# 48 tokens gathered in place of 32, eleven gathers begun in the u pass, gates and first products packed in DRAM by pair of expert tiles

## The chip, the cores and the metric

The kernel runs on one core of a Trainium2 chip. The metric is the device time of one execution in microseconds (us); the time of a kernel is the median of its runs. All data is float32; matrix products run in TensorE's fp32r form with each operand split into a high and a low part, so that one product of full precision is three matmuls (high x high, high x low, low x high).

## What is computed

Two transformer blocks over 256 tokens of width 2048. The change touches only the feed-forward part of the first, a PEER layer with 16384 experts (128 x 128 keys), of which each token picks 128 (8 heads, top 16 of each) with a gate:

```
def peer(xn, wq, subkeys, u, v):
    ...
    idx = e1 * PEER_NKEYS + e2
    gate = jax.nn.softmax(sc, axis=-1).astype(xn.dtype)
    ...
        h = jax.nn.gelu(jnp.einsum('cd,chkd->chk', xc, u[ic]))
        return jnp.einsum('chk,chkd->cd', gc * h, v[ic])
```

`u` and `v` are 16384 x 2048 each, 134 MB each.

## The kernel before

**Two ways through the experts.** Most tokens (`DENSE`, 224 of 256) are done densely. In the *u pass* the 128 tiles of `u` (128 experts each, 1 MB) are multiplied with all dense tokens (`expert_hidden`), the result goes through gelu and to DRAM (`hidden_dram`). In the *v pass* it comes back, is multiplied by a dense table of gates that is zero where an expert was not picked (`weigh`), split into high and low, and multiplied with the 128 tiles of `v` (`expert_mix`). The last `GATHERED` = 32 tokens are done sparsely: their 32 x 128 (token, expert) pairs are laid on 128 partitions, four copies of the 32 tokens, so that 32 *units* of 128 pairs cover them. For each unit GpSimd issues indirect DMAs which fetch 128 rows of `u` (1 MB), VectorE takes the dot product with the token's row (`unit`, L1901, with an accumulator), ScalarE the gelu of all of them (L2689), and then 32 more units fetch rows of `v` and add them, weighted, to `gathered_sum` (L1911). At the end four fp32 matmuls with a 0/1 matrix (`copies_summed`) add the copies into the PSUM banks of the v pass. All 64 units run in the v pass.

**The stream.** SyncE loads weights in halves of a tile (512 KB) into two raw buffers of two halves. ScalarE makes the high part of a half (L2322), VectorE the low part (L1353), into four buffers each; both work three halves ahead of TensorE (`LOOKAHEAD`), and SyncE reloads a half when its low part is done. A half of the u pass is 8 matmuls with a high part as weights and the high and low activations of the dense tokens as moving columns (2 x `DENSE` = 448), then 8 with a low part and the high activations alone (224). A half of the v pass is 12 matmuls of 512 columns whose weights are 128 tokens of the weighed products; the width there does not depend on `DENSE`, since rows up to 256 are filled with zeros.

**Stages of the u pass.** Every engine runs a program in fixed order. In tiles 0 to 47 (`CHOICE_QUADS` = 12 quads of four tiles) VectorE does the top-16 choices between its splits (`choose`, `top16`, `advance`). From tile 48 on, one tile at a time, the dense gates are made, 4 tokens per tile, `GATE_QUADS` = `DENSE` / 16 = 14 quads: VectorE compares indices with iota (`onehots`, L1819, L1822), ScalarE scales the result (`gate_first`, L2599), TensorE multiplies four pairs of one-hot matrices (`gates`), ScalarE and VectorE copy and add the result into `gates_out` (L2607, L1854). The order of VectorE within such a tile is: low part, `sum_hidden` (L1689, every other tile), `sum_gates` of the tile before, `onehots` of the tile after, low part. ScalarE's is: high part, first product or gelu, `copy_gates`, high part, `gate_first` of the tile after, and in some tiles a store of gates. `gates_out` holds two quarters of 64 tokens; each quarter is stored in 8 DMAs, one per tile. The tail of the u pass, tiles 104 to 127, has neither choice nor gates, only the stores of the last quarter in its first eight tiles. When all are stored, GpSimd loads a gain row to all partitions, four copies of the 32 tokens' rows, and the final gain (L2912 to L2915).

**Placement of units.** GpSimd starts a piece of a gather when TensorE is done with a given half (`piece_half`), four pieces of 256 KB per unit; VectorE does unit `u` after the splits of tile `unit_tile(u)`, one unit in 1.8 tiles. There are three gather buffers.

Of the kernel before, what the change touches and what calls it, by code (L numbers as in the profile page):

```python
# [34 lines left out]
P = 128  # L35
# [78 lines left out]
def build(nc, ins, out):  # L114
    ctx = ExitStack()
    with ctx:
# [137 lines left out]
        pair_scale = r_pairs.take(1)  # L254
        r_pairs.take(1)
        copies_summed = r_pairs.take(P)
# [3 lines left out]
        gates_out = r3.take(2 * EXPERT_TILES * QUARTER, "p (b e t) -> p b e t", b=2, t=QUARTER)  # L260
        onehots_at = big_at + 4 * r3.at
# [9 lines left out]
        r3_mix = Region(D)  # L271
        hidden_in = r3_mix.take(2 * N, "p (b n) -> p b n", b=2)
        gates_in = r3_mix.take(2 * N, "p (b q e t) -> p b q e t", b=2, q=T // QUARTER, e=2)
        weighed = r3_mix.take(N)
# [4 lines left out]
        gathered_x = r3_mix.take(D)  # L279
        gathered_rows = r3_mix.take(UNIT_BUFFERS * D, "p (b d) -> p b d", b=UNIT_BUFFERS)  # L280
        gathered_sum = r3_mix.take(D)
        assert r3_mix.at <= 20512
# [4 lines left out]
        gates_dram = nc.dram_tensor("gates_dram", [T // QUARTER, P, EXPERT_TILES, QUARTER], F32)  # L287
        hidden_dram = nc.dram_tensor("hidden_dram", [EXPERT_TILES // 2, P, N], F32)
# [294 lines left out]

        def piece_half(m):

            return 2 + 9 * m // 10

        def unit_tile(u):

            return (piece_half(UNIT_PIECES * u + UNIT_PIECES - 1) + 1) // 2 + 2  # L590

        units_at = {unit_tile(u): u for u in range(UNIT_TILES)}
        assert len(units_at) == UNIT_TILES and max(units_at) < EXPERT_TILES - 2
        dots_tile = unit_tile(UNITS_G - 1) + 1
        assert dots_tile < unit_tile(UNITS_G)
# [6 lines left out]
        def _(sp):  # L602
# [22 lines left out]
            def store_hidden(n, j):  # L625

                sp.wait_ge(gelu_done, 2 * n + (j + 1 + PRIMED))
                sp.dma_start(hidden_dram[bass.ds(2 * n + j, 1)].rearrange("a p n -> p (a n)"), hidden[:, j, :]
                             ).then_inc(hidden_stored[j], 16)

            def load_mix(n, j):
# [6 lines left out]
                sp.dma_start(gates_in[:, j, :, :, :], gates_dram[:, :, bass.ds(4 * n + 2 * j, 2), :].rearrange("q p e t -> p q e t")  # L638
# [50 lines left out]
        def _(pe):  # L689
# [637 lines left out]
        def _(dve):  # L1327
# [555 lines left out]
            for j in range(4):  # L1883
                if j % 2 == 0:
                    sum_hidden(EXPERT_QUADS - 1, j // 2 - 1)
# [1163 lines left out]
```

## Time and profile before

| | |
|---|---|
| median of 3 runs | 2964.53 us (2963.01 to 2964.64) |
| profiled execution, its own time | 2963.21 us |
| its span, first to last instruction | 2961.4 us |
| TensorE busy | 2929.9 us (99%), 16686 matmuls |
| VectorE busy | 2141.8 us (72%) |
| ScalarE busy | 1530.3 us (52%) |
| GpSimd busy | 398.6 us (13%) |
| moved by DMA | 684.56 MB, 231 GB/s on average |
| u pass | from about 437 us to 1128 us |
| v pass | from 1128 us to about 1829 us |

The end of a matmul is modelled and includes its way through the array, so that consecutive matmuls overlap; the pace of TensorE is read from the distance of starts. The share of a DMA window is the time in which an engine has a packet; it can be near 1 before the bytes per second are at their highest.

### The profile page before, as it was taken

The page shows a single profiled execution, that of the slowest core. Times are in us where ns is not written, and L with a number is a line of the kernel's source. Part 1 is how long each engine was busy: PE and PEld are TensorE (multiplying, and loading weights), DVE is VectorE, ACT ScalarE, POOL GpSimd, SP SyncE. Part 2 cuts the span into 40 slices and gives each one's busy share as a digit, 9 for nine tenths or more (in the row PEclk, how much of TensorE's full clock was granted, in tenths as well). Part 3 has the DMA queues.
Part 4 walks back from the last instruction along what each step waited for, and adds up shares of the span by engine and source line. Part 5 has one row for each costly group of instructions (what it writes and reads, how often), then busy time and mean ns, then how long its engine had stood idle before and what let it go on. Part 6 is the DMA issues. An engine that isn't in the chain of part 4 may idle for free.

```text
span 2961.4 us, 46358 instructions
## 1 busy us (share of the span) xinstructions
PE 2929.9 (99%) x16686; PEld 2573.7 (87%) x16686; DVE 2141.8 (72%) x2739; ACT 1530.3 (52%) x2120; POOL 398.6 (13%) x315
## 2 busy tenths in 40 slices
PE   8999999999999999999999999999999999999999
PEld 8887999899999998888888887978889888888887
DVE  5776689977999756777777776775666776777444
ACT  4565534566777644444444444444545555555333
POOL 2000000000000003556556640000000000000000
PEclk9999999999999999999999999999999999999999
DMA  8444546676777989999999995545455555556555
GB/s 285 137 142 149 180 157 208 216 243 213 244 246 255 329 289 317 347 346 351 348 345 346 346 341 173 175 140 171 156 185 183 180 190 192 184 185 196 194 179 184
DMA packets 232763, 684.56 MB, mean 231 GB/s; under 512 B 25613, under 2 KB 62686, under 8 KB 232000
## 3 DMA queue, kind: packets, MB, share of 16 engines
q1 hardware_dynamic: 199552, 583.09, 59.4%
q0 software_dynamic: 23664, 78.15, 7.5%
q10 hardware_dynamic: 9440, 21.93, 2.1%
q8 instruction: 63, 1.03, 0.1%
q14 instruction: 44, 0.36, 0.0%
HBM read 646.28 MB, written 36.49 MB: 231 GB/s over the span
## 4 chain that ended last, share of the span: by engine, by line
PE 84%; DVE 8%; ACT 4%; DMA 2%; issue 2%; ACTq 0%; POOL 0%; SPq 0%; DVEq 0%; POOLq 0%
PE bank L693 83%; DVE low L1353 3%; ACT high L2322 2%; DMA raw<-in_experts_u_t 2%; DVE onehots_both L1819 1%; ACT first_both L2599 1%; PE bank L984 0%; DVE big L1854 0%; DVE big L1698 0%; DVE big L1702 0%; DVE big L1697 0%; DVE big L1689 0%; DVE big L1700 0%; PE bank L783 0%; DMA big<-in_c_onehot_cmp 0%
## 5 line engine op out<-in xcount | busy, mean ns | idle before, releaser
L1353 DVE TENSOR_TENSOR low<-raw,high 128x1024 fp32r<-128x1024 f32 x1008 | 1230.5, 1223 | 655.2 <-ACT high L2322 652.7
L2322 ACT ACTIVATE high<-raw 128x1024 fp32r<-128x1024 f32 x1008 | 1061.3, 1057 | 998.4 <-PE bank L693 901.0
L693 PE MATMUL bank<-act_both,high 128*128 128x448 f32 (+2 forms) x5088 | 1119.3, 348 | 10.9 <-DVE low L1353 8.1
L693 PEld LDWEIGHTS bank<-act_both,high 128*128 128x128 f32 x5088 | 875.7, 190 | 94.0 <-issue 12.9
L693 PE MATMUL bank<-act_both,low 128*128 128x256 f32 (+1 forms) x4240 | 697.1, 278 | 0.0
L693 PEld LDWEIGHTS bank<-act_both,low 128*128 128x128 f32 x4240 | 615.8, 191 | 21.2
L693 PE MATMUL bank<-high,weighed_high 128*128 128x512 f32 x1024 | 399.0, 390 | 0.5 <-DVE weighed_low L1836 0.4
L693 PE MATMUL bank<-high,weighed_low 128*128 128x512 f32 x1024 | 398.4, 389 | 0.0
L693 PE MATMUL bank<-low,weighed_high 128*128 128x512 f32 x1024 | 398.4, 389 | 0.0
L693 PE MATMUL bank<-high,act_both 128*128 128x512 f32 (+1 forms) x960 | 308.7, 392 | 1.4 <-ACT big L2491 1.4
L693 PEld LDWEIGHTS bank<-high,weighed_high 128*128 128x128 f32 x1024 | 192.2, 188 | 41.0 <-issue 1.3
L693 PEld LDWEIGHTS bank<-high,weighed_low 128*128 128x128 f32 x1024 | 192.2, 188 | 40.2
L693 PEld LDWEIGHTS bank<-low,weighed_high 128*128 128x128 f32 x1024 | 192.2, 188 | 39.9 <-issue 0.2
L693 PEld LDWEIGHTS bank<-high,act_both 128*128 128x128 f32 x960 | 180.1, 188 | 37.7 <-issue 1.9
L2927 POOL DMA_INDIRECT big<-in_experts_u,big x128 | 181.3, 1417 | 215.5 <-PE bank L693 199.3
L2927 POOL DMA_INDIRECT big<-in_experts_v_t,big x128 | 188.2, 1470 | 125.3 <-PE bank L693 109.4
L693 PE MATMUL bank<-low,act_both 128*128 128x512 f32 (+1 forms) x480 | 185.4, 386 | 0.0
L693 PE MATMUL bank<-high,ff_high 128*128 128x512 f32 x352 | 137.2, 390 | 0.0
L693 PE MATMUL bank<-low,ff_high 128*128 128x512 f32 x352 | 137.0, 389 | 0.0
L693 PE MATMUL bank<-high,ff_low 128*128 128x512 f32 x352 | 136.9, 389 | 0.0
L2599 ACT ACTIVATE first_both<-onehots_both,taps 128x128 fp32r<-128x128 f32 x224 | 71.8, 391 | 76.3 <-DVE onehots_both L1819 76.3
L693 PE MATMUL bank<-big 128*32 128x128 f32 (+11 forms) x860 | 103.1, 324 | 7.1 <-DMA big<-in_c_onehot_cmp 1.7
(304 smaller groups left out, 2202.2 us busy)
## 6 DMA issues: line engine op xcount, KB each, us to landing
raw<-in_experts_u_t SPq DMA_DIRECT2D x256, 512.0 KB, 4.9
raw<-in_experts_v_t SPq DMA_DIRECT2D x256, 512.0 KB, 6.1
raw<-in_w_up_t SPq DMA_DIRECT2D x176, 512.0 KB, 4.6
raw<-in_w_in_t SPq DMA_DIRECT2D x136, 512.0 KB, 4.0
raw<-in_w_down_t SPq DMA_DIRECT2D x88, 512.0 KB, 4.7
raw<-in_w_out_t SPq DMA_DIRECT2D x64, 512.0 KB, 3.8
raw<-in_peer_wq_t SPq DMA_DIRECT2D x32, 512.0 KB, 3.7
hidden_dram<-big SPq DMA_DIRECT2D x64, 256.0 KB, 3.8
```

The costliest lines, as they stand in the source:

```text
L693: return pe.matmul(out_, lhs_t, rhs, start=start, stop=stop, skip_group_check=True)
L1353: dve.tensor_tensor(low[b][:, :], raw[r][:, HALF * which:HALF * (which + 1)], as_f32(high[b][:, :]), ALU.subtract).then_inc(low_ready[b], 1)
L1819: dve.tensor_tensor(onehots_both[:, c, :, :, :], row(picked_t[:, 0:2, bass.ds(token, FOUR)], P), copies(copies(iota[:, :], FOUR), 2), ALU. ...
L2322: act.activation(high[b][:, :], raw[r][:, HALF * which:HALF * (which + 1)], ACT.Copy).then_inc(high_ready[b], 1)
L2599: m = act.activation(first_high[:, c, t, :], first[:, c, t, :], ACT.Copy, scale=picked_t[:, 2, bass.ds(4 * FOUR * n + (FOUR * j + t), 1)])
L2927: pool.indirect_dma_start(out=gathered_rows[:, b, D // UNIT_PIECES * piece:D // UNIT_PIECES * (piece + 1)], out_offset=None, in_=rows_of, ...
```

## The change

`DENSE` becomes 208, `GATHERED` 48 in two groups: 32 tokens in four copies and 16 tokens in eight copies, each with its own copy of the tokens' rows (`gathered_x`), its own sum and its own 0/1 matrix. That makes 48 units of `u` and 48 of `v`, 96 in place of 64. `GATE_QUADS` becomes 13. A unit is gathered in two pieces of 512 KB. Of the units of `u`, up to `UNIT_TAIL` = 12 are placed in the tail of the u pass, in two of three tiles from tile 110; the list that the expression gives has eleven entries (110, 111, 113, 114, 116, 117, 119, 120, 122, 123, 125). The other 85 go to tiles 1 to 123 of the v pass. In DRAM the first products and the gates lie by pair of expert tiles, 416 floats in a row for each partition. The loads of the token rows and of the gain row come before the tail's units, and the load of the final gain (1 MB) behind unit 35.

```diff
-GATHERED = 32
+TOKEN_GROUPS = [32, 16]
+GATHERED = sum(TOKEN_GROUPS)
 DENSE = T - GATHERED
-COPIES = P // GATHERED
-UNITS_G = P // COPIES
+UNITS_G = GATHERED
 UNIT_BUFFERS = 3
-UNIT_PIECES = 4
+UNIT_PIECES = 2
+UNIT_FROM, UNIT_TAIL = 109, 12
...
+        gathered_x = [Region(0).take(D), Region(r3.at).take(D)][:len(TOKEN_GROUPS)]
...
-        gates_dram = nc.dram_tensor("gates_dram", [T // QUARTER, P, EXPERT_TILES, QUARTER], F32)
-        hidden_dram = nc.dram_tensor("hidden_dram", [EXPERT_TILES // 2, P, N], F32)
+        gates_dram = nc.dram_tensor("gates_dram", [EXPERT_TILES // 2, P, 2 * DENSE], F32)
+        hidden_dram = nc.dram_tensor("hidden_dram", [EXPERT_TILES // 2, P, 2 * DENSE], F32)
...
+        tail_tiles = [t for t in range(UNIT_FROM, EXPERT_TILES - 2) if t % 3 != UNIT_FROM % 3][:UNIT_TAIL]
+        UNITS_V = UNIT_TILES - len(tail_tiles)
...
+            if u < len(tail_tiles):
+                return tail_tiles[u]
+            return EXPERT_TILES + 1 + u // UNITS_G + (u - len(tail_tiles)) * (EXPERT_TILES - 5) // UNITS_V
+
+        def unit_half(u, piece):
+
+            h = 2 * unit_tile(u) - 5 + piece * 2 // UNIT_PIECES
+            return half("experts_u_t", h) if h < 2 * EXPERT_TILES else half("experts_v_t", h - 2 * EXPERT_TILES)
...
-                    for q in range(4):
-                        mm(bank[:, 4 + q, :], copies_summed, gathered_sum[:, N * q:N * q + N], start=False, stop=False)
+                    for g in range(len(TOKEN_GROUPS)):
+                        for q in range(4):
+                            mm(bank[:, 4 + q, :], copies_summed[:, g, :], gathered_sum[g][:, N * q:N * q + N], start=False, stop=False)
...
+            def gather_step(tile):
+
+                if UNIT_FROM - 2 <= tile < UNIT_FROM - 2 + len(TOKEN_GROUPS):
+                    g = tile - (UNIT_FROM - 2)
+                    dve.wait_ge(subkeys_rows_gain_landed, 16 * (2 + X_LOADS))
+                    dve.tensor_tensor(gathered_x[g], gathered_x[g], gathered_rows[:, UNIT_BUFFERS - 1, :], ALU.mult
+                                      ).then_inc(gathered_x_ready, 1)
...
-                act.dma_start(gates_dram[q, :, at, :], gates_out[:, q % 2, at, :]).then_inc(gates_stored[q % 2], 16)
+                tokens = quarter_tokens(q)
+                to = gates_dram[EXPERT_TILES // 2 // GATE_PIECES * piece:EXPERT_TILES // 2 // GATE_PIECES * (piece + 1), :,
+                                2 * QUARTER * q:2 * (QUARTER * q + tokens)]
+                act.dma_start(to.rearrange("a p n -> p a n"),
+                              gates_of(q)[:, at, :].rearrange("p (a e) t -> p a (e t)", e=2)).then_inc(gates_stored[q % 2], 16)
...
-            for b in range(2):
-                pool.wait_ge(gates_stored[b], 16 * GATE_PIECES * 2)
+            pool.wait_ge(gates_stored[0], 16 * GATE_PIECES * 2)
             pool.dma_start(gathered_rows[:, UNIT_BUFFERS - 1, :], ins["ffn_norm"].partition_broadcast(P)).then_inc(subkeys_rows_gain_landed, 16)
...
+            for c in range(SLOTS):
+                pool.wait_ge(gates_done[c], 2 * GATE_QUADS + PRIMED)
+            for g, tokens in enumerate(TOKEN_GROUPS):
+                for r in range(P // tokens):
+                    pool.dma_start(gathered_x[g][tokens * r:tokens * (r + 1), :], resid[group_at[g]:group_at[g] + tokens, TT - 1, :]
+                                   ).then_inc(subkeys_rows_gain_landed, 16)
```

## Rows read from the trace of the kernel before

**Rows 1.** The chain that ended last, by line, share of the span.

```profile
PE bank L693 83%; DVE low L1353 3%; ACT high L2322 2%; DMA raw<-in_experts_u_t 2%; DVE onehots_both L1819 1%; ACT first_both L2599 1%; PE bank L984 0%; DVE big L1854 0%; DVE big L1698 0%; DVE big L1702 0%; DVE big L1697 0%; DVE big L1689 0%; DVE big L1700 0%; PE bank L783 0%; DMA big<-in_c_onehot_cmp 0%
```

**Rows 2.** Windows: stretch, length; busy us of PE, PEld, DVE, ACT, POOL; clock; DMA share; GB/s.

```profile
561.00:617.00 56.00, 56.00 (x358) 53.20 (x357) 55.17 (x51) 35.73 (x39) 0.00 (x0) 1.00 0.73 232
617.00:697.00 80.00, 80.00 (x509) 76.00 (x508) 47.05 (x52) 49.47 (x59) 5.91 (x12) 1.00 0.75 241
...
698.00:1002.00 304.00, 304.00 (x1983) 289.87 (x1982) 275.88 (x301) 224.97 (x437) 0.00 (x0) 1.00 0.75 249
...
1030.00:1045.00 15.00, 15.00 (x97) 14.24 (x96) 9.05 (x10) 8.82 (x10) 0.00 (x0) 1.00 1.01 387
...
1060.00:1075.00 15.00, 12.92 (x74) 12.02 (x73) 6.39 (x6) 7.16 (x9) 0.00 (x0) 0.89 0.93 313
...
1075.00:1125.00 50.00, 50.00 (x319) 47.49 (x318) 29.34 (x28) 25.93 (x31) 0.00 (x0) 1.00 0.80 263
...
1140.00:1450.00 310.00, 310.00 (x1369) 256.68 (x1369) 238.98 (x233) 135.49 (x143) 179.26 (x127) 1.00 0.98 348
```

**Rows 3.** Timeline of TensorE: start, us, operation, times, in five short stretches.

```profile
902.36 0.65 PE L693 MATMUL bank<-first_both,onehots_both 128*128 128x256 f32 x4
902.85 1.79 PE L693 MATMUL bank<-act_both,high 128*128 128x448 f32 x8
...
1107.48 1.80 PE L693 MATMUL bank<-act_both,high 128*128 128x448 f32 x8
1109.12 1.04 PE L693 MATMUL bank<-act_both,low 128*128 128x224 f32 x8
1110.01 1.80 PE L693 MATMUL bank<-act_both,high 128*128 128x448 f32 x8
...
1819.59 3.60 PE L693 MATMUL bank<-big 128*128 128x512 f32 x8
...
1978.60 1.95 PE L693 MATMUL bank<-big 128*128 128x64 f32 x16
```

**Rows 4.** Timeline of all engines in the choices: a low part and the half that uses it.

```profile
565.87 1.22 DVE L1353 TENSOR_TENSOR low<-raw,high 128x1024 fp32r<-128x1024 f32 x1
...
568.78 0.38 PE L693 MATMUL bank<-act_both,high 128*128 128x448 f32 x1
```

**Rows 5.** Timeline of all engines in the gate tiles; in brackets idle before, and releaser.

```profile
698.12 0.64 PE L693 MATMUL bank<-first_both,onehots_both 128*128 128x256 f32 x4
698.24 1.22 DVE L1819 TENSOR_TENSOR onehots_both<-taps,iota 128x1024 fp32r<-128x1024 f32 x1
...
703.64 0.65 PE L693 MATMUL bank<-first_both,onehots_both 128*128 128x256 f32 x4
...
904.12 1.22 DVE L1819 TENSOR_TENSOR onehots_both<-taps,iota 128x1024 fp32r<-128x1024 f32 x1
...
905.37 0.41 ACT L2599 ACTIVATE first_both<-onehots_both,taps 128x128 fp32r<-128x128 f32 x1 [1.14 <-DVE onehots_both L1819]
...
906.56 1.04 ACT L2322 ACTIVATE high<-raw 128x1024 fp32r<-128x1024 f32 x1
...
907.64 1.23 DVE L1353 TENSOR_TENSOR low<-raw,high 128x1024 fp32r<-128x1024 f32 x1 [0.33 <-ACT high L2322]
...
909.91 1.22 DVE L1819 TENSOR_TENSOR onehots_both<-taps,iota 128x1024 fp32r<-128x1024 f32 x1
...
999.17 1.22 DVE L1819 TENSOR_TENSOR onehots_both<-taps,iota 128x1024 fp32r<-128x1024 f32 x1
...
1002.05 0.65 PE L693 MATMUL bank<-first_both,onehots_both 128*128 128x256 f32 x4
```

**Rows 6.** DMA issues of 1045 to 1062 us: queue, times, KB each, us to landing.

```profile
raw<-in_experts_u_t SPq DMA_DIRECT2D x5, 512.0 KB, 14.6
...
big<-in_final_norm POOLq DMA_DIRECT2D x1, 1024.0 KB, 19.1
```

**Rows 7.** Line L1901, VectorE's instruction of a unit of u: ns min/median/max.

```profile
L1901 DVE SCALAR_TENSOR_TENSOR big<-big x32: 2282/2284/2290, 1155.6 to 1460.3; 128x2048 f32<-128x2048 f32 x32
```

More of the change, by code:

```diff
@@ L1870, in _ @@
                 for j in range(4):
-                    gate_tile(q, n0, j, q if j else (q - 1 if q else None))
+                    gate_tile(q, n0, j, q if j else (q - 1 if q else None), last=n0 == GATE_QUADS - 1 and j == 3)
                 if not last_q:
@@ L1875, in _ @@
                             gate_tile(q, n, j, q)
-            assert GATE_QUADS == QUARTER_QUADS * (T // QUARTER - 1) + 2
-            for j in range(4):
-                gate_tile(T // QUARTER - 1, GATE_QUADS - 1, j, T // QUARTER - 1, last=j == 3)
+            for n in range(QUARTER_QUADS * (T // QUARTER - 1) + 1, GATE_QUADS):
+                for j in range(4):
+                    gate_tile(T // QUARTER - 1, n, j, T // QUARTER - 1, last=n == GATE_QUADS - 1 and j == 3)
             sum_gates(T // QUARTER - 1, GATE_QUADS, -1)
-            with dve.Fori(0, EXPERT_QUADS - CHOICE_QUADS - GATE_QUADS - 1) as n:
-                for j in range(4):
-                    split_tile_low("experts_u_t", n + (CHOICE_QUADS + GATE_QUADS), j)
@@ L1883, in _ @@
-            for j in range(4):
-                if j % 2 == 0:
-                    sum_hidden(EXPERT_QUADS - 1, j // 2 - 1)
-                split_low(half("experts_u_t", 2 * j + LOOKAHEAD, EXPERT_QUADS - 1))
-                if j == 3:
-                    weigh_low(0, 0)
-                split_low(half("experts_u_t", 2 * j + LOOKAHEAD + 1, EXPERT_QUADS - 1))
-                if j == 2:
-                    weigh(0, 0)
-            sum_hidden(EXPERT_QUADS - 1, 1)
             def unit(u):
-                b, used = u % UNIT_BUFFERS, u // UNIT_BUFFERS
+                b, used, column = u % UNIT_BUFFERS, u // UNIT_BUFFERS, u % UNITS_G
@@ new lines, in _ @@
+            for tile in range(4 * (CHOICE_QUADS + GATE_QUADS), EXPERT_TILES):
+                n, j = tile // 4, tile % 4
+                if n < EXPERT_QUADS - 1:
+                    split_tile_low("experts_u_t", n, j)
+                else:
+                    if j % 2 == 0:
+                        sum_hidden(n, j // 2 - 1)
+                    split_low(half("experts_u_t", 2 * j + LOOKAHEAD, n))
+                    if j == 2:
+                        dve.wait_ge(gates_stored[1], 16 * GATE_PIECES * 2)
+                        for ap in (weighed_high, weighed_low):
+                            dve.memset(as_f32(ap.rearrange("p b (e t) -> p (b e) t", e=2)[:, :, DENSE:]), 0.0)
+                    elif j == 3:
+                        weigh_low(0, 0)
+                    split_low(half("experts_u_t", 2 * j + LOOKAHEAD + 1, n))
+                    if j == 2:
+                        weigh(0, 0)
+                gather_step(tile)
@@ L1914, in _ @@
+            sum_hidden(EXPERT_QUADS - 1, 1)
             for n in range(EXPERT_QUADS):
```

150 lines of the change are left out of this document (82 added, 68 removed).

## The prediction

> **What bounds the kernel now.** I read the chain of work first: 83% of it is one line, TensorE's matmul helper, and the next, VectorE's low part, has 3% [rows 1]. Then windows by stage. From 561 us to the end of the v pass TensorE is busy in practically every microsecond [rows 2], so a shorter matmul can pay, but only where nobody else stands close behind. Who does is read from VectorE and DMA in the same windows: VectorE is busy 55.17 of 56 us at the end of the choices, 47.05 of 80 after them, 275.88 of 304 in the gate tiles; DMA is at 0.75 in the gate tiles, at 1.01 and 387 GB/s while the last quarter of gates is stored, and at 0.98 and 348 GB/s in the v pass [rows 2]. One stretch lost time: 1060 to 1075, TensorE busy 12.92 of 15 and the clock at 0.89, part of it at 1.2 in place of 2.4 GHz. That is 2.1 us idle and 0.11 x 15 = 1.7 us of clock, 3.8 us, just after GpSimd's loads of the two gain rows and the tokens' rows (1 MB each): the weight halves beside it took 14.6 us to land [rows 6]. The timeline of TensorE gives the price of a half, the timeline of all engines the gate tiles.
>
> **The matmuls of the u pass.** A half starts at 1107.48, its low part at 1109.12, the next half at 1110.01 [rows 3]: 1.64 us for 8 matmuls of 448 columns (205 ns each), 0.89 us for 8 of 224 (111 ns), 2.53 us in all; the long run of the gate tiles, below, gives 2.518. The change makes them 416 and 208. The wide ones should follow their columns: 32 columns at 2.4 GHz are 13.3 ns, 8 x 13.3 = 0.107 us per half. The narrow ones may not. Elsewhere 16 matmuls of 64 columns with a full 128x128 weight take 1.95 us [rows 3]; less some 0.27 for the way of the last one through the array that is 1.68 / 15 = 112 ns each, though their columns are 27 ns (the same sum for the narrow ones: (1.04 - 0.27) / 7 = 110). The 224-column ones pass at the same 111 ns. So some 110 ns looks like what it takes to change weights, and 208 columns save nothing. The ends: 0 (the 64-column row) and 16 columns = 6.7 ns x 8 = 0.053 us per half. I take 0, since two widths so far apart share one pace. Saved per half: 0.107 us, 27 us over 256 halves if TensorE alone set the pace.
>
> The Trainium skill, page "TensorE: Matmul & The Clock Gate", section "LDWEIGHTS (loading the stationary operand)", says the same: a weight load takes time by its 128 columns, 128 / 1.2 = 107 ns, whatever streams past. The section "Back-to-back issue gap" of that page prices an isolated gap by the columns alone, and by it the narrow matmuls would save too.
>
> **Choices, tiles 0 to 47.** Up to about 617 us VectorE has no idle time [rows 2] and its program doesn't get shorter but for the sums of first products (448 to 416 columns, under 1 us together). TensorE can't be ahead of it. It can only eat its lead: the low part that ends at 565.87 + 1.22 is used at 568.78, 1.7 us later [rows 4]. After 617, 32 halves at 0.107 are 3.4 us. Gain: 1.7 + 0.6 + 3.4 = 5.7.
>
> **Gate tiles.** This is where I expect most of the gain to vanish. There TensorE takes 5.526 us per tile: (1002.05 - 703.64) / 54 [rows 5], which is two halves and 0.49 for the four gate matmuls (902.36 to 902.85 [rows 3]), so 2.518 for a half. VectorE's one-hot comparisons go at (999.17 - 698.24) / 54 = 5.573 us [rows 5], slower than TensorE. Their lead over the gate matmuls that use them falls from 703.64 - 698.24 = 5.40 to 1002.05 - 999.17 = 2.88 us. What drives them is a loop of VectorE and ScalarE in which TensorE has no part: comparison at 904.12, ScalarE waited 1.14 us for it and starts the scaled copies at 905.37, then its high part at 906.56, VectorE waited 0.33 for that and makes the low part at 907.64, adds, and compares again at 909.91 [rows 5]. Nothing in this loop shrinks but the add of first products (0.03 us every other tile: 0.017 per tile). The lead can't fall below comparison plus copies, about 2.5 us. So 52 tiles take 52 x 5.556 less the 2.9 us of lead, 286.0, against 52 x 5.526 = 287.4 before: a gain of 1.4, where TensorE alone would gain 52 x 2 x 0.107 = 11.1. The other bound is that the loop has slack that I don't see: 11.1. I take 1.4, because in that window no wait of VectorE or ScalarE on TensorE stands against the loop. The four tiles that lose their gates go from 5.526 to 2 x (2.518 - 0.107) = 4.82: 2.8. The 32 stores of gates remain 32; those of q 0 to 2 go in rows of 512 B, the last in rows of 128 B. Their issue lies in that loop (some 0.1 us), 20 in place of 24 inside the stage.
>
> **Tail, the 24 tiles from 104.** 48 x 0.107 = 5.1. VectorE takes on a unit of 2.28 us [rows 7] in 11 tiles; with two splits of 1.23 and half a sum it is at some 5.0 us in such a tile of 4.83 and 2.8 in the third, which its lead hides. The two products with the gain row, once under the v pass, are now at tiles 107 and 108, and VectorE waits there for 1 + 12 loads of GpSimd. These start when the store of tile 103 has landed, about 5 us into tile 104, and move 3 MB like the cluster before, whose last load took 19.1 us [rows 6]; with 12 issues I put the end at 26.6 us after the start of tile 104. VectorE arrives at 19.2. Behind the wait are the low parts of half 219 and on: 26.6 + 2.28 + 1.23 = 30.1 against the 26.6 at which TensorE wants it. 3.5 us idle, and a clock fall like that of 1060 (1.7): 5.2 in place of the 3.8 us lost before. Bounds: 0 (landing early) to 10. Then the gathers: per tile of 4.83 us 1.05 MB of weights, 0.11 of first products, two thirds of 1.05 of rows: 1.85 MB, 384 GB/s, where the nearest stretch had 387 at a share of 1.01 [rows 2]. That is the edge; I count 2.5 us, from 0 to 6.3 (at 348 / 0.98 = 355 GB/s a tile takes 5.22, 0.39 x 16). Sum of the tail against before: 5.1 - (5.2 + 2.5 - 3.8) = +1.2.
>
> **The v pass.** Its 3072 matmuls keep their form: 0. Twenty-one units more (85 for 64) are 21 x 2.3 = 48 us of VectorE's time, which has 71 us idle in 310 [rows 2]: hidden; the smaller weigh operations pay for their second instruction. If the cover is gone the low parts come late, at most by one unit. GpSimd issues 192 gathers for 256. DMA: in 10.88 us (two tiles) weights 2.10 MB, packed operands 0.43 for 0.52, rows 1.45 for 1.17: 365 GB/s for 348. Larger rows than 512 B speak for it, the share of 0.98 against. I count 1 us lost, between 0 and 19 (355 GB/s: 2.8% of 684 us). The load of the final gain, 1 MB alone, is hidden. At the end 4 fp32 matmuls more: eight records at 0.43 us make four of them [rows 3], 3.4 us on the path.
>
> **Sum.** 5.7 + 1.4 + 2.8 + 1.2 - 1 - 3.4 = 6.7 us off the profiled execution's own 2963.2 (span 2961.4), 2956.5. The median of the runs is 1.3 above that execution, so 2957.8; I say 2958.
>
> **The rivals.**
>
> DMA is the limit (slower). Place: tail and v pass; it decides as soon as the kernel can't be served over 355 GB/s for long. The tail loses 3.8 more, the v pass 19 in place of 1: 2958 + 22 = 2980. For it: shares of 0.98 to 1.01 at 348 to 387 GB/s. Against: the share is full long before the bytes stop rising (387), and TensorE never waited in the v pass. The middle of this case is 2970, half of it within 0.2% of before. The Trainium skill, page "DMA: Bandwidth & Descriptors", section "Where 436 GB/s comes from", puts the HBM side of one core at some 358 GB/s, and by it this case would come about; its section "Measured (HBM→SBUF, 128 partitions, SWDGE, issued from GpSimd)" has 425 for one core alone, and the row with 387 sides with that.
>
> The gate loop isn't binding: +9.7, 2948. For it: TensorE was never idle there. Against: the falling lead [rows 5].
>
> The narrow matmuls follow their columns: 0.053 x (32 + 56 halves) = 4.7: 2953.
>
> No larger stall: loads land before tile 107 and the gathers fit: up to 7.7 less, 2951.
>
> The change does nothing in sum: 2964.5, inside the spread of the above.
>
> **How the numbers follow.** Forecast case (2953 to 2964) 0.45, gate loop or columns 0.17, no stall 0.13, DMA 0.25. A measurement here can tell 0.2%, 5.9 us. Faster by more than that (under 2958.6): 0.5 of the first, all of the next two: 0.52. Within: 0.45 of the first and half of the DMA case: 0.33. Slower: 0.15. The range leaves out the upper part of the DMA case and little below: 2946 to 2974; the forecast's own is 2953 to 2964.
>
> **What would show it.** Halves in the tail start every 2.41 us, with 8 narrow matmuls still at 0.11 (2.36 would be the other case). In the gate tiles TensorE's period stays near 5.55 and it waits for the low part or for the one-hots, in all about 10 us. TensorE idle once near tile 107 with VectorE waiting on a DMA. GB/s near 380 in the last 16 tiles of the u pass. v pass from first matmul to last still about 701 us plus 3.4. I am wrong if gate tiles take 5.32, or the v pass grows by more than 8 us.

## The result and the profile after

The changed kernel takes 2996.05 us (median of 4 runs, 2990.71 to 2998.17) against 2964.59 us (4 runs, 2963.01 to 2964.68): a ratio of 1.0104, 95% interval 1.0092 to 1.0115. It is 31 us slower, where I had said 6.5 us faster. Its profiled execution took 2998.17 us, with a span of 2996.4 us.

I laid the two traces over each other by the starts of the 256 halves of the u pass and of the 3072 matmuls of the v pass. "Ahead" is how much earlier the changed kernel gets there.

| point | before, us | after, us | ahead | predicted |
|---|---|---|---|---|
| tile 48 (half 96), end of the choices | 693.08 | 686.49 | 6.6 | 5.7 |
| tile 100 (half 200), end of its gate tiles | 980.36 | 972.96 | 7.4 | 7.1 |
| tile 104 (half 208) | 1002.53 | 992.37 | 10.2 | 9.9 |
| tile 109 (half 218) | 1027.83 | 1016.50 | 11.3 | 10.9 |
| tile 110 (half 220) | 1032.88 | 1039.09 | -6.2 | not told apart |
| first matmul of the v pass | 1127.96 | 1128.61 | -0.6 | 8.7 |
| last matmul of the v pass | 1829.16 | 1864.16 | -35.0 | 4.3 |

So the change works as foreseen for 109 tiles, loses 17.5 us between the halves of tiles 109 and 110, gets 5.6 of that back by the end of the u pass (the kernel before has its own stall there [rows 2]), and loses 34 us in the v pass.

The chain that ended last, by line, shows only that time went to other places than before [rows 1]:

```profile
PE bank L714 64%; DVE low L1375 4%; DMA raw<-in_experts_v_t 3%; DMA raw<-in_experts_u_t 1%; ACT high L2359 1%; DVE big L1922 1%; DMA big<-resid 1%; DVE big L1911 1%; PE bank L1005 0%; DVE big L1720 0%; DVE big L1724 0%; DVE big L1719 0%; DVE big L1722 0%; DVE big L1801 0%; DVE big L1803 0%
```

Windows of the changed kernel (columns as in [rows 2]):

```profile
698.00:992.00 294.00, 290.64 (x1922) 284.35 (x1921) 261.19 (x286) 214.35 (x412) 0.00 (x0) 1.00 0.77 251
1006.00:1012.00 6.00, 6.00 (x43) 5.97 (x42) 4.52 (x6) 3.43 (x5) 6.00 (x13) 1.00 1.06 327
1012.00:1018.00 6.00, 6.00 (x40) 5.96 (x39) 0.00 (x0) 1.34 (x2) 3.07 (x4) 1.00 1.06 289
1018.00:1024.00 6.00, 1.07 (x9) 0.89 (x8) 0.00 (x0) 1.06 (x1) 0.94 (x1) 0.82 1.04 219
1024.00:1030.00 6.00, 0.00 (x0) 0.00 (x0) 0.00 (x0) 0.00 (x0) 0.00 (x0) 0.50 1.02 218
1075.00:1125.00 50.00, 48.55 (x317) 47.60 (x316) 40.37 (x41) 25.35 (x30) 14.80 (x11) 1.00 0.94 341
1140.00:1450.00 310.00, 305.51 (x1303) 245.91 (x1303) 241.84 (x267) 128.54 (x139) 109.74 (x74) 0.99 0.96 352
```

From 1018 to 1030 nearly everything stands still at a DMA share over 1.0 and only 218 GB/s; the clock falls from 2.4 to 1.2 GHz (0.50) as TensorE stands. Timeline of all engines around it (matmuls left out but for the first after the stall):

```profile
997.53 0.38 ACTq L2672 DMA_DIRECT2D gates_dram<-big  x1
...
1005.84 0.54 POOL L2963 DMA_DIRECT2D big<-in_ffn_norm  x1 [365.82 <-DMA gates_dram<-big]
1006.37 5.78 POOL L2968 DMA_DIRECT2D big<-resid  x12
...
1010.61 1.23 DVE L1375 TENSOR_TENSOR low<-raw,high 128x1024 fp32r<-128x1024 f32 x1 [0.40 <-ACT high L2359]
...
1022.84 1.06 ACT L2359 ACTIVATE high<-raw 128x1024 fp32r<-128x1024 f32 x1 [9.51 <-DMA raw<-in_experts_u_t]
...
1030.54 2.29 DVE L1930 TENSOR_TENSOR big<-big 128x2048 f32<-128x2048 f32 x1 [18.71 <-DMA big<-resid]
...
1034.65 1.75 PE L714 MATMUL bank<-act_both,high 128*128 128x416 f32 x4 [15.58 <-DVE low L1375]
```

The reader is to see four times: the last store of the gates of quarter 2 issued at 997.53, GpSimd let go by it at 1005.84, VectorE done with everything ahead of the x step at 1011.84, and the x step at 1030.54. The DMA view of 1006 to 1030 says what was in flight (KB each, median us to landing):

```profile
raw<-in_experts_u_t SPq DMA_DIRECT2D x3, 512.0 KB, 17.6
big<-in_ffn_norm POOLq DMA_DIRECT2D x1, 1024.0 KB, 8.6
big<-resid POOLq DMA_DIRECT2D x4, 256.0 KB, 11.0
big<-resid POOLq DMA_DIRECT2D x8, 128.0 KB, 15.9
gates_dram<-big ACTq DMA_DIRECT2D x3, 128.0 KB, 26.5
```

In the v pass the first thing to see is the pace. Timeline of TensorE in the kernel before, then in the changed one:

```profile
1240.25 0.39 PE L693 MATMUL bank<-high,weighed_high 128*128 128x512 f32 x1
...
1241.61 0.39 PE L693 MATMUL bank<-high,weighed_high 128*128 128x512 f32 x1
```

```profile
1239.62 0.39 PE L714 MATMUL bank<-high,weighed_high 128*128 128x512 f32 x1
...
1241.02 0.39 PE L714 MATMUL bank<-high,weighed_high 128*128 128x512 f32 x1
```

Six matmuls take 1.36 us before (227 ns each) and 1.40 after (233 ns), nobody waiting. An undisturbed v tile of 24 takes 5.44 us before and 5.57 to 5.60 after, from the first tile to the last: about 18 us over the pass. The second thing is some ten gaps of 0.5 to 3 us each between pairs of tiles, 12 to 13 us in sum. Some 3 us of that are clock and not waiting: behind the gaps at tiles 36 and 86 seven matmuls each start 0.43 us apart, and the granted clock is 0.50 (1.2 GHz) from 1337 to 1339 us, after TensorE had stood for 2.57 us. The third was foreseen: the fp32 matmuls, now sixteen records in 7.03 us against eight in 3.60 [rows 3].

### The profile page after: what moved, and what is told of

It is laid out like the page before. It is cut to its first block, busy times and chain, and to the rows that moved or that the text cites. A ratio compares the mean times of both kernels' runs of the same rounds, so it can differ in the third digit from the quotient of the medians.

```text
span 2996.4 us, 46333 instructions
## 1 busy us (share of the span) xinstructions
PE 2935.5 (98%) x16678; PEld 2579.6 (86%) x16678; DVE 2191.0 (73%) x2842; ACT 1515.1 (51%) x2101; POOL 345.7 (12%) x283
## 3 DMA queue, kind: packets, MB, share of 16 engines
q0 software_dynamic: 31856, 112.76, 10.4%
## 4 chain that ended last, share of the span: by engine, by line
PE 66%; issue 14%; DVE 10%; DMA 6%; ACT 2%; POOL 1%; SPq 1%; ACTq 0%; DVEq 0%; POOLq 0%
PE bank L714 64%; DVE low L1375 4%; DMA raw<-in_experts_v_t 3%; DMA raw<-in_experts_u_t 1%; ACT high L2359 1%; DVE big L1922 1%; DMA big<-resid 1%; DVE big L1911 1%; PE bank L1005 0%; DVE big L1720 0%; DVE big L1724 0%; DVE big L1719 0%; DVE big L1722 0%; DVE big L1801 0%; DVE big L1803 0%
## 5 line engine op out<-in xcount | busy, mean ns | idle before, releaser
L714 PE MATMUL bank<-act_both,high 128*128 128x416 f32 (+2 forms) x5088 | 1094.8, 343 | 29.0 <-DVE low L1375 25.3
L714 PE MATMUL bank<-high,weighed_high 128*128 128x512 f32 x1024 | 406.7, 397 | 8.4 <-DVE weighed_low L1860 8.3
L714 PE MATMUL bank<-high,weighed_low 128*128 128x512 f32 x1024 | 405.5, 396 | 0.0
L714 PE MATMUL bank<-low,weighed_high 128*128 128x512 f32 x1024 | 405.3, 396 | 0.0
L2983 POOL DMA_INDIRECT big<-in_experts_v_t,big x96 | 158.7, 1653 | 237.7 <-PE bank L714 212.8
L2983 POOL DMA_INDIRECT big<-in_experts_u,big x96 | 142.6, 1485 | 270.9 <-PE bank L714 256.4
L714 PE MATMUL bank<-big 128*32 128x128 f32 (+12 forms) x868 | 105.6, 324 | 6.9 <-ACT big L2427 1.6
L1911 DVE SCALAR_TENSOR_TENSOR big<-big 128x2048 f32<-128x2048 f32 x48 | 109.7, 2285 | 0.0
```

Of the source, the lines that this page charges most:

```text
L714: return pe.matmul(out_, lhs_t, rhs, start=start, stop=stop, skip_group_check=True)
L1911: dve.scalar_tensor_tensor(gathered_rows[:, b, :], gathered_rows[:, b, :], 1.0, gathered_x[g], ALU.mult, ALU.mult, accum_out=pair_dots[:, ...
L2983: pool.indirect_dma_start(out=gathered_rows[:, b, D // UNIT_PIECES * piece:D // UNIT_PIECES * (piece + 1)], out_offset=None, in_=rows_of, ...
```

## The experiments

Each ratio below is to the kernel before, run beside it on the same chip; its median there was 2962 to 2964 us.

**Place of the weight tiles.** `weighed_high` is what the v pass loads as weights, 128 columns (512 bytes) at a time. Its place in the tile `big` went from float 4608 to float 10272. The 6144 floats of the three gather buffers, which now lie ahead of it, change nothing in the remainder; the three operand tiles there, whose pairs went from 512 to 416 columns, do: 10272 floats are 41088 bytes, 128 past a multiple of 256. All such remainders here are counted from the start of `big`.

a1_align, the changed kernel:

```diff
         weighed = r3_mix.take(2 * DENSE)
+        r3_mix.take(480)
```

> The changed kernel with one edit: 480 floats are left free ahead of weighed_high, so that this tile starts at float 10752 of big (a multiple of 512 floats, as 4608 was in the kernel before) and not at 10272. Everything else, transfers and waits included, is that of the changed kernel. Theory 'place' (a weight tile that starts off a 512-byte boundary makes each v matmul start later): the interval between matmuls of the v pass goes back from about 232 ns to 227 ns, some 5 ns x 3072 = 15 us, so 2996 becomes about 2980; the stall near tile 108 of the u pass stays. Rival 'contention' (the larger gather rows and longer VectorE work share the memory with TensorE): the interval stays at 232 and the time at about 2996.

Measured: 2986.48 us (6 runs), 1.0081 (1.0067 to 1.0095). b1_shift32, the kernel before:

```diff
         weighed = r3_mix.take(N)
+        r3_mix.take(32)
```

> The kernel before with one edit: 32 floats are left free ahead of weighed_high, so that it starts at float 4640 of big and not at 4608, with the same remainder as in the changed kernel (128 bytes past a multiple of 512). Theory 'place': its v matmuls go from 227 ns to about 232 ns and its time from 2964.6 to about 2980. Rival 'contention': nothing in the traffic changes, so 227 ns and 2964.6 within 0.2%.

Measured: 2981.64 us, 1.0065 (1.0051 to 1.008). Timeline of TensorE in b1_shift32, then in a1_align:

```profile
1239.81 0.39 PE L694 MATMUL bank<-low,weighed_high 128*128 128x512 f32 x1
...
1241.20 0.39 PE L694 MATMUL bank<-low,weighed_high 128*128 128x512 f32 x1
```

```profile
1240.16 0.39 PE L715 MATMUL bank<-high,weighed_high 128*128 128x512 f32 x1
...
1241.52 0.39 PE L715 MATMUL bank<-high,weighed_high 128*128 128x512 f32 x1
```

1.39 us for six in the first, 1.36 in the second. The v pass of b1_shift32 is 719.9 us from first to last matmul, against 701.2: 32 empty floats cost 18.7 us, with not a byte of traffic changed and no wait of TensorE added. "Contention" is out. (`gathered_sum`, which lies behind the weight tiles, moved with them; e1 below rules it out.) a1_align has its 227 ns back, but not 15 us: its gaps grew. Its v pass is still 723.9 us. So a second cause is at work, stronger when TensorE is faster.

**Loads or gathers in the tail of the u pass, and where VectorE waits.** Both on a1_align:

```diff
 # a2_x_later
-UNIT_FROM, UNIT_TAIL = 109, 12
+UNIT_FROM, UNIT_TAIL = 115, 8
 # a3_no_tail
-UNIT_FROM, UNIT_TAIL = 109, 12
+UNIT_FROM, UNIT_TAIL = 109, 0
```

> The kernel of a1_align, and the x steps of VectorE moved from tiles 107 and 108 to tiles 113 and 114; 8 units remain in the tail of the u pass (tiles 115 to 125) in place of 12, the other 4 go to the v pass. The 13 loads that GpSimd issues stay where they are, after the gates are stored. Theory 'in-order wait' (VectorE stands 18.7 us behind those loads and the low halves queue behind it): the wait is gone or below 3 us, the u pass ends some 12 us earlier, about 12 us off a1_align's time. Rival 'the DMA engines themselves' (2 MB of x, 1 MB of gain, the last gate stores and the stream do not fit at once): ScalarE waits for raw in place of VectorE, TensorE stands still for 10 us or more between tiles 104 and 114 all the same, and at most 5 us come back.

> The kernel of a1_align with no unit in the tail of the u pass: all 96 units stand in the v pass, the x steps stay at tiles 107 and 108, and the first gathers are issued in the v pass. It tells the loads from the gathers. If the 13 loads and the gate stores make the stall, VectorE still waits over 12 us at tile 107 and TensorE loses about as much as before. If the four gathers issued right behind the loads make it, the wait falls to 5 us or less. The v pass then holds 96 units, about one in 1.3 tiles, at 2.3 us each beside a tile of 5.45 us of matmuls: if VectorE or the gathers were too much for a v tile, its tiles would pass 5.6 us.

(The program's rule leaves out every third tile and stops at tile 125, so that 11 of the 12 and 7 of the 8 units get a place in the tail. "84" and "88" units in the v pass are 85 and 89.)

a2_x_later: 2986.99 us, 1.0081 (1.0067 to 1.0096). Between halves 218 and 222 TensorE loses 8.7 us against the kernel before, where a1_align lost 15.1, now behind ScalarE's waits for raw; the u pass ends 4.6 us earlier than in a1_align, not 12. Both theories have a part of it: VectorE's standing cost some 6 us, the crowd at the DMA engines 9. The time is that of a1_align although the u pass gained 4.6 us: the v pass, with four units more, is 3.3 us longer (727.2 us).

a3_no_tail: 2999.78 us, 1.0129 (1.0114 to 1.0143). No gather is near, and the half at tile 110 still starts 15.9 us later against before than the one ahead of it: the gathers have no part in the stall. Windows of a3_no_tail:

```profile
1018.00:1024.00 6.00, 2.37 (x16) 2.17 (x14) 0.00 (x0) 1.06 (x1) 0.00 (x0) 1.00 1.05 241
1024.00:1030.00 6.00, 0.00 (x0) 0.00 (x0) 0.00 (x0) 1.06 (x1) 0.00 (x0) 0.56 0.98 232
```

The v pass with 96 units takes 734.9 us, 11 more than a1_align's with 85.

**Size of the gathers' pieces, tokens, bytes.** Edits of a1_align; c3_32_tokens has 320 in place of 480 floats, which puts `weighed_high` at the same float 10752.

```diff
 # c1_pieces4, c2_pieces1
-UNIT_PIECES = 2
+UNIT_PIECES = 4        # c2_pieces1: 1
 # c3_32_tokens
-TOKEN_GROUPS = [32, 16]
+TOKEN_GROUPS = [32]
-UNIT_FROM, UNIT_TAIL = 109, 12
+UNIT_FROM, UNIT_TAIL = 109, 0
 # c5_half_gather_v
-out=gathered_rows[:, b, D // UNIT_PIECES * piece:D // UNIT_PIECES * (piece + 1)],
+out=gathered_rows[:, b, D // UNIT_PIECES * piece:D // UNIT_PIECES * (piece + 1) - (512 if u >= UNITS_G + UNIT_BUFFERS else 0)],
```

> The kernel of a1_align with every gathered row fetched in 4 pieces of 2 KB, as in the kernel before, in place of 2 pieces of 4 KB. Same bytes, twice the packets of the gathers. Theory 'DMA rate' (84 units stand in the v pass where 64 stood; 1.97 MB a tile in 5.44 us is 362 GB/s, and a1_align moved 351 to 360 GB/s at a DMA share of 0.96 to 0.98, so the pieces of v arrive late and TensorE loses 19 us in some 12 places): with the rate of the kernel before, 346 to 349 GB/s at 0.98, each v tile would take 1.97 MB / 348 GB/s = 5.66 us, and the v pass would lose about 27 us and not 19: about 8 us slower than a1_align. Rival 'bursts' (a 0.5 MB piece holds back the stream's tile behind it): smaller pieces interleave better and 5 us or more come back.

> The kernel of a1_align with every gathered row fetched in one piece of 8 KB. 'DMA rate': somewhat fewer packets, so the same time as a1_align or up to 5 us less. 'Bursts': 1 MB at once holds back the stream twice as long; 5 us or more slower than a1_align.

> The changed code with 32 gathered tokens as before (64 units, all in the v pass, none in the tail), DRAM packed by pair of expert tiles, x loads and x step where the change has them (tiles 104 to 107 of the u pass), and weighed_high on a multiple of 512 floats. It is the packing, the larger pieces of 4 KB and the earlier x loads without the 16 tokens more. If the losses come from the 16 tokens (32 units more), the v pass takes 701 us as before, at a lower DMA share than 0.98, and the time is 2962 within 0.3%, a few us less if the early x step costs nothing; if the packing or the order of the tail makes them, it is 2970 or more.

> The kernel of a1_align, but from the 52nd unit on (tile 59 of the v pass) each piece fetches 2 KB of its 4 KB: it leaves out half of those rows' columns, which keep old values. VectorE's and GpSimd's instructions are the same in number and length. 'DMA bytes': up to tile 59 TensorE loses about 8 us as in a1_align, after it nothing but the 3.4 us of the four fp32 matmuls and the end (a1_align: 14 us), so about 10 us less in all. Rival 'VectorE' (units of 2.3 us in order ahead of the low halves): the stalls after tile 59 stay, 14 us.

| kernel | median, us | ratio (95%) | v pass, first to last matmul, us |
|---|---|---|---|
| a1_align, 2 pieces | 2986.48 | 1.0081 (1.0067 to 1.0095) | 723.9 |
| c1_pieces4 | 2970.88 | 1.0023 (1.0014 to 1.0033) | 711.5 |
| c2_pieces1 | 2993.84 | 1.0114 (1.0095 to 1.0132) | 730.9 |
| c3_32_tokens | 2962.79 | 0.9995 (0.9986 to 1.0004) | 701.7 |
| c5_half_gather_v | 2977.49 (one run) | | 717.4 |

My theory of a DMA rate fell: 4 pieces are 15.6 us faster, not 8 slower. The rival, bursts, said 5 or more, and 5 or more the other way for one piece: c2_pieces1 is 7.4 us slower. Windows of 1140 to 1800 us: the kernel before, the changed one, a1_align, c1_pieces4, c2_pieces1:

```profile
1140.00:1800.00 660.00, 659.64 (x2910) 545.88 (x2910) 505.85 (x462) 289.04 (x305) 367.37 (x254) 1.00 0.97 343
```

```profile
1140.00:1800.00 660.00, 651.66 (x2782) 525.22 (x2782) 513.81 (x524) 272.78 (x293) 248.98 (x159) 0.99 0.96 351
```

```profile
1140.00:1800.00 660.00, 647.78 (x2833) 531.99 (x2834) 522.04 (x535) 276.78 (x297) 262.05 (x161) 1.00 0.97 355
```

```profile
1140.00:1800.00 660.00, 655.42 (x2881) 541.11 (x2880) 530.40 (x541) 282.65 (x303) 478.07 (x329) 1.00 0.99 363
```

```profile
1140.00:1800.00 660.00, 644.12 (x2807) 527.68 (x2806) 517.45 (x528) 275.09 (x294) 147.72 (x81) 0.99 0.95 352
```

The same units are fetched, in pieces of 1 MB, 512 KB and 256 KB, and the DMA engines move 352, 355 and 363 GB/s. Between 4 and 2 pieces the packets are no answer: the queue of the gathers has 31856 packets in the changed kernel and 34928 in c1_pieces4 over the whole execution (the expectation's "twice" was wrong). In both, 25776 of them carry 4096 bytes; the 3072 more in c1_pieces4 carry 4 bytes each. What is cut finer is the issue. In c2_pieces1 the packets differ too: 13056 of 8192 bytes. What the issues do to the stream shows in the slow halves of v: the median landing of a raw half is 6.6 us in a1_align and in c1_pieces4, but 21 of 256 take over 9 us in the first and 5 in the second. How a late half becomes a gap is seen in the timeline of the changed kernel:

```profile
1324.89 0.33 SPq L657 DMA_DIRECT2D big<-hidden_dram  x1
1325.32 0.38 SPq L659 DMA_DIRECT2D big<-gates_dram  x1
1328.57 1.06 ACT L2359 ACTIVATE high<-raw 128x1024 fp32r<-128x1024 f32 x1 [5.74 <-DMA raw<-in_experts_v_t]
...
1330.81 0.55 DVE L1851 TENSOR_TENSOR big<-big 128x384 f32<-128x384 f32 x1
...
1334.73 0.58 DVE L1860 TENSOR_TENSOR weighed_low<-big,weighed_high 128x416 fp32r<-128x416 f32 x1
...
1335.45 0.49 PE L714 MATMUL bank<-high,weighed_high 128*128 128x512 f32 x1 [2.57 <-DVE weighed_low L1860]
```

ScalarE stands 5.74 us until a raw half lands; behind it on VectorE come a low part, then the weighing, a unit, a low part, and only then the low part of the weighed products, for which TensorE stands 2.57 us at the start of tile 36. All gaps but the half-clock stretches lie at starts of even tiles, where a new pair's weighed products are first used. In c5_half_gather_v the v pass loses 12.7 us up to tile 64 (a1_align 8.3), and from there to tile 126 nothing (a1_align 10.9), with VectorE's work unchanged. Windows of 1476 to 1750 us, a1_align and c5_half_gather_v:

```profile
1476.00:1750.00 274.00, 266.93 (x1164) 218.80 (x1163) 212.85 (x202) 113.11 (x121) 114.34 (x68) 0.99 0.96 350
```

```profile
1476.00:1750.00 274.00, 274.00 (x1211) 226.95 (x1210) 224.70 (x212) 118.17 (x126) 116.45 (x71) 1.00 0.89 299
```

Late transfers are the cause, VectorE's units only pass them on. This is one execution of a kernel that fetches half of the rows' columns there, and it halves the bytes together with the size of an issue, so it does not tell the two apart. c3_32_tokens shows the packing by pairs, the loads of x in the u pass and even two pieces to be free with 64 units: 336 GB/s, v pass 701.7 us. Its x step, with 1 MB of x in place of 2, stalls TensorE for 4.9 us; the kernel before has about as much further on [rows 2].

**The stall again, the rule for the place, and the pieces alone.** d1, d2 and d3 are edits of c1_pieces4; d4 is one of the changed kernel (`UNIT_PIECES = 4` only). d3_rem256 has `r3_mix.take(32)` in place of 480. d2_late_4 is `UNIT_FROM, UNIT_TAIL = 115, 8`; d1_paced is that, and on GpSimd:

```diff
                 for r in range(P // tokens):
+                    hb, _, _, done = half("experts_u_t", 2 * (UNIT_FROM - 10) + sum(P // n for n in TOKEN_GROUPS[:g]) + r)
+                    pool.wait_ge(half_used[hb], done + 1 + PRIMED)
                     pool.dma_start(gathered_x[g][tokens * r:tokens * (r + 1), :], ...
```

> The kernel of c1_pieces4 (changed kernel, weighed_high on a multiple of 512 floats, gathered rows in 4 pieces of 2 KB), with the x steps at tiles 113 and 114, 8 units in the tail of the u pass (tiles 115 to 125), and each of the 12 loads of x held back until another half tile of the u pass is used (halves 210 to 221), so that they don't stand at the DMA engines all at once. Theory 'burst of loads' (ffn_norm, 12 loads of x and the last gate stores, over 3 MB at 220 to 300 GB/s and a DMA share of 1.0, hold the stream back for 24 us): the half at tile 110 (half 220) keeps the 10 us that it is ahead of the kernel before, where c1_pieces4 had lost 13.7 us by then; the v pass starts some 8 to 11 us earlier than in c1_pieces4, and the time is about 2961 (2957 to 2966), level with the kernel before or a little under it. Rival 'total' (the bytes don't fit wherever they stand): the loss moves to later halves and the v pass starts no more than 3 us earlier than in c1_pieces4: 2968 or more.

> As d1_paced without the holding back: the 12 loads of x are issued in one go at tile 104 as in the changed kernel, but VectorE asks for them at tile 113. 'Burst of loads': ScalarE still waits for raw behind them, and TensorE loses 6 to 9 us by half 222 (a2_x_later: 9.2 us); d1_paced is 4 us or more better. 'In-order wait' (only VectorE's standing was the cost): as d1_paced within 2 us.

> The kernel of c1_pieces4 with weighed_high at float 10304 of big, 256 bytes past a multiple of 512, in place of 10752. If what matters is that a weight column block of 512 bytes starts on a multiple of 512 bytes, the v matmuls go to 229 to 238 ns again, 15 us slower than c1_pieces4 (2986); if a multiple of 256 bytes is enough, they stay at 227 ns and the time at 2971.

> The changed kernel with one edit: gathered rows in 4 pieces of 2 KB in place of 2 of 4 KB; weighed_high stays at float 10272. If place and pieces are two causes that add up: v matmuls at about 232 ns, the jumps of the v pass mostly gone, about 2971 + 15 = 2986 us, and the v pass 711 + 15 = 726 us long. If the slower matmuls leave enough slack for the stream, pieces matter less here: the v pass 3 to 5 us shorter still, as 232 ns needs 6 GB/s less.

| kernel | median, us | ratio (95%) |
|---|---|---|
| d1_paced | 2962.87 (11 runs) | 1.0005 (0.9996 to 1.0014) |
| d2_late_4 | 2967.40 | 1.0013 (1.0004 to 1.0023) |
| d3_rem256 | 2971.54 | 1.0027 (1.0017 to 1.0038) |
| d4_pieces4_only | 2986.23 | 1.0084 (1.0068 to 1.0099) |

d3: at 256 bytes past a multiple of 512 the matmuls keep 227 ns; so 0 and 256 are good places and 128 is a bad one (384 was not tried). d4: the time is 2986 as for two causes that add up, with 232 ns; its v pass of 722.9 us is that of the other expectation (726 less 3 to 5). d2 is 3.5 us faster than c1_pieces4 and d1 4.5 faster than d2, but neighbours among these intervals overlap, so the traces have to tell. Between halves 218 and 222 TensorE loses 14.1 us in c1_pieces4, 8.8 in d2 (6 to 9 expected) and 5.6 in d1; the v pass starts 3.6, 8.6 and 10.2 us earlier than before. So asking for x later (with four units fewer in the tail) is worth some 5 us there, and spreading the loads 3.2 us at half 222, of which 1.6 is left at the v pass. The rest of the 4.5 us lies in v passes of 713.8 (d2) and 707.4 us (d1) that run the same program: two profiled executions of one v pass can be 6 us apart, and no difference of that size between single v passes is safe. d1 also starts the v pass only 6.6 us earlier than c1_pieces4, where 8 to 11 were expected. Windows of d1_paced:

```profile
1006.00:1024.00 18.00, 15.30 (x102) 14.84 (x100) 5.51 (x6) 5.37 (x7) 3.40 (x7) 1.00 1.04 269
1024.00:1034.00 10.00, 8.74 (x47) 8.60 (x48) 5.47 (x5) 4.14 (x5) 0.97 (x2) 0.83 1.10 286
1140.00:1800.00 660.00, 658.20 (x2899) 543.88 (x2900) 543.74 (x551) 283.88 (x304) 490.12 (x343) 1.00 1.00 370
```

Spreading leaves 5.6 us lost between halves 218 and 222: the stretch is still at a share of 1.04 to 1.10 and under 290 GB/s.

**What was still open.** e1_high_only is c1_pieces4 with the tiles apart (`offset=big_at + 4 * (r3_mix.at + n * (2 * N + 224))`, no 480 floats ahead); e2_paced_no_tail is d1_paced with `UNIT_TAIL` 0.

> The kernel of c1_pieces4 with the two weight tiles placed apart: weighed_high stays at float 10272 of big (128 bytes past a multiple of 256), weighed_low moves to float 11520 (a multiple of 128 floats). Of the three matmuls on one bank two load weighed_high and one loads weighed_low. If each load from a displaced tile costs its own matmul, two thirds of the 5 ns come: a mean interval of 230 ns, the v pass 10 us longer than c1_pieces4's 711 us; if the displaced place of something else that moved with these tiles (gathered_sum, in all kernels so far) were the cause, 227 ns.

> The kernel of d1_paced with no unit in the tail of the u pass: all 96 units stand in the v pass in place of 89 (the list of tail tiles has 7 entries in d1_paced, and 11 in the changed kernel, not the 8 and 12 that I wrote before). It shows what the tail units are worth once the loads of x are spread. d1_paced moved 368 to 372 GB/s in the v pass at a DMA share of 0.99 to 1.00, so 7 MB more should not fit: 7.3 MB / 370 GB/s = 20 us more of transfers in v, against slack of about 1% (7 us); the u pass gains 2 to 4 us of it. Expected 2962.9 + 8 to 14, so 2971 to 2977. If the DMA engines had room left, within 3 us of d1_paced.

e1_high_only: 2987.98 us, 1.009 (1.0073 to 1.0107), with 233 ns on average, 232.5 to 235 by kind of matmul, the one that loads `weighed_low` from its good place included, and a v pass of 727.3 us. So `weighed_high` alone is enough for the whole loss, not for two thirds, and `gathered_sum`, at a multiple of 256 bytes here, has no part in it. How one displaced load slows its neighbour, and what `weighed_low` alone would do, was not tried.

e2_paced_no_tail: 2987.48 us, 1.0097 (1.0074 to 1.012), 24.6 us over d1_paced, more than the 8 to 14 expected. Its windows:

```profile
1140.00:1800.00 660.00, 639.66 (x2788) 520.87 (x2787) 534.76 (x544) 272.92 (x292) 546.56 (x360) 1.00 1.00 366
```

The v pass can't take 96 units: share 1.00, 366 GB/s, TensorE idle 20 of 660 us, v pass 733.9 us. With 89 it is 707.4 in d1 and 713.8 in d2. The seven units in the u pass's tail are worth 20 to 26 us in the v pass and cost under 3 in the u pass. With 96 units the size of the pieces no longer matters: a3_no_tail, with pieces of 512 KB, has a v pass of 734.9 us and this window:

```profile
1140.00:1800.00 660.00, 641.30 (x2794) 524.97 (x2793) 534.24 (x546) 273.63 (x293) 269.79 (x181) 0.99 0.98 368
```

**What "place" means.** The program's allocation, the same before and after, puts `big` at byte 114816 of each partition, which is itself 128 past a multiple of 256, and `high`, `low` and `act_both` have the same remainder. In these addresses the good places of `weighed_high` lie 128 and 384 bytes past a multiple of 512, and the bad one, both in the changed kernel and in b1_shift32, 256 past. `act_both` and `ff_high` serve as weights from the good remainder elsewhere in the program, and their matmuls of 512 columns start every 227 to 228 ns as well. But those with `high` as the weights and `act_both` moving take 231 ns from the same remainder, so it is not all that counts. The runs don't tell whether the address itself counts or its distance from the moving operand (`high`, `low`), which never moved.

## Why the prediction was wrong, step by step

**Where the 31 us are.** The changed kernel less c1_pieces4, place and pieces together, is 25.2 us; c1_pieces4 less d1_paced, the burst of loads and the x step's tile, is 8.0; d1_paced is level with the kernel before. (These are differences of medians from several chips, on which the kernel before had 2962 to 2964.6.) By the medians the place costs 15.4 us with small pieces (d4 less c1) and 9.6 with large ones (the changed kernel less a1_align). The v passes, one profiled execution of each kernel, do not show this difference: there the place costs 11.4 us with small pieces and 11.6 with large ones, and large pieces cost 12.6 us at the good place (a1_align less c1) and 12.4 at the bad one, so that place and pieces add up to the 24.0 us between the changed kernel and c1. What both cases show is that the slower pace, 17.8 us over the pass, costs only some 11.5: the gaps are 6 us shorter beside it. I take it that a slower TensorE leaves the stream more time; nothing tests that alone.

**"Its 3072 matmuls keep their form: 0."** This is the step that failed first. Form and count are the same; the place of the weights is not, and the term put at 0 measured about 18 us of undisturbed time (5.57 to 5.60 us a tile for 5.44). None of my rivals had it, and no row of before could have priced it. What could be seen is that the diff changes the sizes in front of `weighed_high`. The prediction's own sign of being wrong, a v pass that grows by more than 8 us, came with 34.3.

**"DMA: I count 1 us lost, between 0 and 19."** The bytes were right (365 GB/s foreseen, 363 reached by c1_pieces4). The size was wrong: the term measured 723.9 - 701.2 - 3.4 = 19.3 us in a1_align, at the bound of 19, and about 13 in the changed kernel, beside the slower pace. What the sum left out is the size of a gather's issue, which it named only as fewer issues for GpSimd (192 for 256): it is 12 of the 19 us. With small pieces the term is 711.5 - 701.2 - 3.4 = 6.9 us. The larger rows in DRAM, which the prediction had speak for a small term, are a different thing; c3_32_tokens has them with 64 units, and its v pass is neither shorter nor longer (701.7 us).

**"5.2 in place of the 3.8."** VectorE reached the x step at 1011.84, tile 104 + 19.5 us, as foreseen (19.2). The loads landed at 38.2 us and not at 26.6. Of these 11.6 us, 8.5 are the start: I let GpSimd go 5 us into tile 104, but that is when the last store of quarter 2 was issued (997.53), and it took 8.3 us to land. Only 3.1 are a longer cluster, 24.7 us for 21.6. Every later half was then behind VectorE: 15.6 us idle, and most of the rest of the 17.5 at a clock of 1.2 GHz. A second part of this step was wrong: it made VectorE's wait the whole cost. a2_x_later takes that wait away and still loses 8.7 us, because the raw halves themselves come late (17.6 us to land in the view of 1006 to 1030).

The Trainium skill, page "SBUF — State Buffer", section "Door 1: The DMA port swizzle (why `[64,N]` ≈ `[32,N]`)", says that a transfer's rate goes by how many of 16 ports its partitions reach, and that 32 partitions in a row reach 8 and 16 reach 4. The 218 GB/s at a full share between 1024 and 1030, with the x copies from 32 and 16 partitions in flight, agree with it in direction; no run here has the same bytes from other partitions.

**Right.** Choices 6.6 (5.7). Gate tiles 0.8 in 52 tiles (1.4): their period is (972.35 - 696.64) / 50 = 5.514 us, where TensorE alone would need 2 x 2.413 + 0.49 = 5.316, so it waits 10 us in all, as written (the window of 698 to 992 shows only 3.4 us idle). The four tiles without gates 2.8 (2.8). The gathers in the tail: from half 220 to the v pass the changed kernel makes up 5.6 us and a3_no_tail, without them, 8.0, so they cost 2.4 (2.5). The 380 GB/s foreseen there did not come, though: 356 between 1045 and 1125 us, at a share of 0.97. Timeline of TensorE in the gate stage and in the tail:

```profile
696.64 0.53 PE L714 MATMUL bank<-first_both,onehots_both 128*128 128x256 f32 x3
...
972.35 0.71 PE L714 MATMUL bank<-first_both,onehots_both 128*128 128x256 f32 x4 [0.15 <-ACT first_both L2636]
...
1097.05 1.70 PE L714 MATMUL bank<-act_both,high 128*128 128x416 f32 x8
1098.58 1.04 PE L714 MATMUL bank<-act_both,low 128*128 128x208 f32 x8
1099.46 1.70 PE L714 MATMUL bank<-act_both,high 128*128 128x416 f32 x8
```

A half takes 2.41 us, with the 8 narrow matmuls still at (1099.46 - 1098.58) / 8 = 0.11 us: the floor for changing weights stands. The fp32 matmuls cost 3.43 us (3.4).

**The rival "DMA is the limit"** gave 2980 with 355 GB/s as the ceiling. The direction was that of the result, the mechanism only partly: 370 GB/s at a share of 1.00 were held for 660 us in d1_paced, and large pieces are no ceiling of 355 either, since a3_no_tail moved 368 with them. The mean rate follows what is asked; how late single halves come is what differs. (A slip in the rival without a stall: 7.7 less than 2957.8 is 2950, not 2951; nothing hangs on it.) The Trainium skill, page "DMA: Bandwidth & Descriptors", section "Where 436 GB/s comes from", has some 358 GB/s as the HBM side of one core; the 370 of d1_paced are over it, and the measurement decides.

## What to carry to other kernels

A change that alters the size of one tile in a hand-laid region moves all that lie behind it: look where the weights of the hottest matmuls come to lie, keep the remainder by 256 bytes that they had, and time a matmul where it changes. Where two streams share the DMA engines near their limit, cut the less urgent one into small issues (12 us here with 85 units, nothing with 96, where the bytes are too many), and spread bursts over the tiles ahead of the one that asks for them. And read the wait in front of a load as issue plus landing of the transfer it waits for: an in-order engine behind a load that starts 8 us late pays for all of it.

## What the runs showed of the hardware that I had not expected

- fp32r matmuls of 512 columns with a 128x128 weight start every 227 ns when the weight tile lies a multiple of 256 bytes from the start of `big` (remainders 0 and 256 of 512 tried) and every 232 to 233 ns when it lies 128 bytes past a multiple of 512. `big` itself starts at byte 114816. `weighed_high` displaced alone is enough.
- The share of time in which DMA engines have a packet says little of what they move: 218 GB/s at 1.02 (copies between partitions of SBUF and 128-byte rows), 370 at 1.00, 387 at 1.01 [rows 2].
- With 85 units, gathers issued as 1 MB, 512 KB and 256 KB give v passes of 730.9, 723.9 and 711.5 us; the last two have the same packets of data. Of the stream's 256 halves, 21 take over 9 us to land beside 512 KB and 5 beside 256 KB, at the same median of 6.6.
